# Another order ahead of the gathered rows, and the expert choices cut into pieces

## The reference

```python
# first block
xn = rms_norm(h, mix_norm_w); q, f, i, g, lru_x, lru_gate = split(xn @ w_in)
o_hg  = hgrn2_mix(q, f, i, g)      # linear attention with gates, in chunks of 32 tokens:
        # b = cumsum(log f); q*exp(b), k*exp(-b), k*exp(b_last - b); a state goes from chunk to chunk
o_lru = rglru_mix(lru_x, lru_gate) # conv of 4 taps, sigmoid gates, h_t = a_t h_{t-1} + b_t, times gelu
h += concat(o_hg, o_lru) @ w_out
h += (silu(gate) * up) @ w_down    # gate, up = split(rms_norm(h) @ w_gate_up), 2816 wide
x  = rms_norm(h)
# second block
shift1, scale1, gate1, shift2, scale2, gate2 = silu(c) @ ada_w + ada_b
h = rms_norm(x) * (1 + scale1) + shift1;  r_q, r_k, r_v, r_g, s_q, s_k, s_v = split(h @ w_in)
y_ret = group_norm(retention(rope(r_q), rope(r_k), r_v)) * silu(r_g)        # 8 heads of 64
y_sb  = rms_norm(stick_breaking(rms_norm(s_q), rms_norm(s_k), s_v))         # 8 heads of 64
x += gate1 * (concat(y_ret, y_sb) @ w_out)
h2 = rms_norm(x) * (1 + scale2) + shift2
# PEER: for each of 8 heads, 2 lists of 128 scores -> best 16 of each -> best 16 of the 256 sums
qry = h2 @ w_query; top_s, top_i = top_k(qry . sub_keys, 16)
best_s, best_c = top_k(top_s[0][:, None] + top_s[1][None, :], 16)
act = gelu(h2 . expert_down[ids]) * softmax(best_s)       # 16384 experts, 128 per token
x += gate2 * sum(act * expert_up[ids])
```

## Time and profile before

| | |
|---|---|
| median of 3 runs | 1166.53 us (1166.04 to 1167.21) |
| profiled execution, own time | 1169.27 us |
| its span, first to last instruction | 1167.4 us |
| PE busy | 1029.6 us (88%) |
| DVE busy | 856.1 us (73%) |
| ACT busy | 419.9 us (36%) |
| POOL busy | 282.2 us (24%) |
| HBM read | 376.61 MB, 324 GB/s over the span |
| mean granted TensorE clock | 0.956 of full speed |

### The profile page before, as it was taken

One profiled execution on the slowest core, in us unless ns is written; L12 is line 12 of the kernel. 1 busy time (PEld: TensorE's weight loads), 2 busy tenths in 40 slices (PEclk: granted clock), 3 DMA queues, 4 the chain that ended last, 5 costly groups with the idle time before them and its releaser, 6 DMA issues.

```text
span 1167.4 us, 14402 instructions
## 1 busy us (share of the span) xinstructions
PE 1029.6 (88%) x5158; PEld 720.7 (62%) x5158; DVE 856.1 (73%) x1784; ACT 419.9 (36%) x835; POOL 282.2 (24%) x260
## 2 busy tenths in 40 slices
PE   6999999999999998988899998787788668768887
PEld 6988999999999876975465554333233223323343
DVE  5987689998868884585658777677866776776655
ACT  4654544445446663343123322222221222222112
POOL 0000000000000000044344554544354344334430
PEclk9999999999999999999899999988898899889899
DMA  9532449978937433498899999999999999999994
GB/s 356 208 127 91 148 180 350 362 290 316 325 104 288 163 108 117 192 360 332 350 421 420 421 422 421 421 422 421 422 422 421 421 421 422 421 421 421 421 422 200
DMA packets 67895, 378.61 MB, mean 324 GB/s; under 512 B 7536, under 2 KB 7920, under 8 KB 35056
## 3 DMA queue, kind: packets, MB, share of 16 engines
q0 software_dynamic: 36864, 268.45, 55.6%
q1 hardware_dynamic: 29808, 106.09, 25.1%
q10 hardware_dynamic: 1152, 3.15, 0.8%
HBM read 376.61 MB, written 1.05 MB: 324 GB/s over the span
## 4 chain that ended last, share of the span: by engine, by line
PE 47%; DMA 30%; DVE 14%; ACT 5%; issue 4%; POOL 0%; SPq 0%; POOLq 0%; DVEq 0%; ACTq 0%
DMA xn<-in_peer,idsb 23%; PE pb L929 7%; PE pb L431 7%; PE pb L428 7%; PE pb L932 7%; DMA ring_sb<-in_peer,idsb 5%; PE pb L456 4%; DVE ring_lo L1452 3%; PE pb L813 2%; PE pb L643 2%; PE pb L884 1%; DVE ring_sb L2062 1%; PE pb L473 1%; PE pb L475 1%; PE pb L474 1%
## 5 line engine op out<-in xcount | busy, mean ns | idle before, releaser
L929 PE MATMUL pb<-ring_sb,arena 128*128 128x512 f32 x274 | 151.9, 638 | 83.1 <-ACT arena L1391 83.1
L2062 DVE CUSTOM_DVE_ANT_0 ring_sb<-ring_sb,arena 128x1024 f32<-128x1024 f32 x137 | 164.3, 1223 | 54.2 <-DMA ring_sb<-in_peer,idsb 54.1
L2134 POOL DMA_INDIRECT ring_sb<-in_peer,idsb x137 | 153.5, 1121 | 208.3 <-PE pb L932 186.3
L428 PE MATMUL pb<-xhi,whi 128*128 128x256 f32 x736 | 190.8, 293 | 0.8 <-ACT xhi L1012 0.5
L431 PE MATMUL pb<-xlo,whi 128*128 128x256 f32 x736 | 186.0, 287 | 0.5 <-DVE xlo L1671 0.3
L2134 POOL DMA_INDIRECT arena<-in_peer,idsb x38 | 40.8, 1074 | 558.8 <-DVE idsb L2041 496.6
L1386 ACT ACTIVATE arena<-arena 128x4 f32<-128x4 f32 (+2 forms) x71 | 14.5, 205 | 408.6 <-DVE arena L2062 408.6
L1452 DVE TENSOR_TENSOR ring_lo<-ring_sb,whi 128x1024 fp32r<-128x1024 f32 x126 | 147.5, 1220 | 13.3 <-ACT whi L985 13.3
L932 PE MATMUL pb<-ring_sb,arena 128*128 128x512 f32 x274 | 149.6, 629 | 0.0
L428 PEld LDWEIGHTS pb<-xhi,whi 128*128 128x128 f32 x736 | 142.6, 194 | 5.3 <-issue 3.2
L431 PEld LDWEIGHTS pb<-xlo,whi 128*128 128x128 f32 x736 | 142.7, 194 | 4.4 <-issue 2.7
(11 more groups left out here) (367 smaller groups left out, 1801.6 us busy)
## 6 DMA issues: line engine op xcount, KB each, us to landing
ring_sb<-in_ada SPq DMA_DIRECT2D x48, 512.0 KB, 5.2
ring_sb<-in_w_gu SPq DMA_DIRECT2D x44, 512.0 KB, 6.5
ring_sb<-in_w_in SPq DMA_DIRECT2D x38, 512.0 KB, 7.5
ring_sb<-in_w_down SPq DMA_DIRECT2D x22, 512.0 KB, 5.6
ring_sb<-in_w_out SPq DMA_DIRECT2D x16, 512.0 KB, 3.4
ring_sb<-in_w_q SPq DMA_DIRECT2D x8, 512.0 KB, 3.6
whi_rows<-in_w_q SPq DMA_DIRECT2D x6, 512.0 KB, 7.6
ring_sb<-in_peer,idsb POOLq DMA_INDIRECT x137, 22.5
```

The costliest lines, as they stand in the source:

```text
L428: e.matmul(o, hi_w(u)[:, c], xh(k), start=start, stop=False, skip_group_check=skip)
L929: mm = e.matmul(pb[4 + 2 * tile][:, :], dgr[col % 8], o[:, 1024:1536], start=begin, stop=end)
L2062: e.tensor_tensor_reduce(o, o, h2t[tile], 1.0, 0.0, MUL, ADD, aa[:, col:col + 1]).then_inc(*VD.up(("dot", col)))
L2134: e.indirect_dma_start(rows_at[s], None, peer, bass.IndirectOffsetOnAxis(ap=idsb[:, col:col + 1], axis=0)).then_inc(s_row[s], 16)
```

## The change

It moves work and cuts the choices; the arithmetic of the result is the same but for the order of a few sums.

- Start: ten `keep_clock` matmuls on the first input tile as soon as it is there, in place of eight behind the constants.
- `ADDED`: in n0 and n1 DVE adds slices 1 to 5, in n2 slices 1 to 3; PE adds the others by matmuls.
- First block: on DVE the memsets and the scan go ahead of the second query product, on ACT exp(b) goes last; on PE the gate matmuls go ahead of the intra-chunk ones; on DVE state steps 5 and 6 go ahead of the root's product and the LRU's product; ACT writes the high parts of the LRU's output ahead of the last sigmoid, DVE the low parts ahead of the last gate product.
- `residual`: the last two units are split after the last additions (ACT: one ahead, one behind).
- The plain sums go into the middle of U_rk's product.
- Retention: U_rg's first product goes ahead of the first group sum, its second ahead of the first mean; means and norms of the two halves are taken one by one, among the pieces of the output product; the gate is multiplied in ahead of the norm's factor (`gated`), which is then two products of 512 in place of four of 256.
- First choice: two banks, one for each list; the queries' additions go ahead of the normalised product; `match_replace` goes ahead of the first `decode`.
- Choice 1 is spread over dots 0 to 7; `second_add` stands behind dot 2, `second_norm` behind dot 6. Choices 2 to 15 become eight pieces each, one behind each of eight dots (`piece_at`).
- Groups: four of 2, 58 of 4, two of 2, twelve of 1. The places of queries and scores move by one group, scores one group closer.
- ACT loads the tables for gelu and for exp by hand in the first rows.

```diff
+        GR = [range(i, i + 2) for i in range(0, 8, 2)] + [range(i, i + 4) for i in range(8, 240, 4)]
+        GR += [range(i, i + 2) for i in range(240, 244, 2)] + [range(i, i + 1) for i in range(244, 256)]
+        second_at = {4: 0, 5: 1, 10: 2}
+        query_at = {6: (3, 0), 7: (3, 1)} | {4 * h - 8 + j: (h, j) for h in range(4, 8) for j in range(2)}
+        piece_at = {c + j: (n, j) for n, c in [(2, 16), (3, 28)] + [(n, 16 * n - 24) for n in range(4, 16)] for j in range(8)}
+        choose_at = {7: 2, 10: 3} | {4 * n - 3: n for n in range(4, 16)}
+        ADDED = {"n0": 6, "n1": 6, "n2": 4}
...
 # PE, sums
-                e.wait_ge(*AN.at((name, "sq", 7)))
-                e.matmul(pb[b][:, 0:T], c_("ones"), sq[:, 2 * T:3 * T], start=False, stop=True).then_inc(*PN.up(name))
+                for k in range(ADDED[name], KD):
+                    e.wait_ge(*AN.at((name, "sq", k)))
+                    mm = e.matmul(pb[b][:, 0:T], c_("ones"), one_(sq, sq_slot(k)), start=False, stop=k == KD - 1)
+                mm.then_inc(*PN.up(name))
...
+            e.wait_ge(s_x[0], 16)
+            keep_clock(10, hT[:, 0:128])
             e.wait_ge(s_cst, 16)
-            sums("n0", (8, 8), (AN, ("n0", "ln")))
+            sums("n0", (0, 8), (AN, ("n0", "ln")))
...
-            plain_sums()
-            gemm(U_rk[2:4], ("rk", 1), (AR, ("rk", "raw", 1)), mid=lambda: rope_turn("rk", 0))
+            gemm(U_rk[2:4], ("rk", 1), (AR, ("rk", "raw", 1)), mid=lambda: (plain_sums(), rope_turn("rk", 0)))
...
             ret_scores(2)
-            group_sum(AS, ("o", 0), AS, half(tmp, 0))
-            ret_out(0)
-            gemm(U_rg[0:2], ("rg", 0), (AR, ("rg", 0)), mid=lambda: group_sum(AS, ("o", 1), AS, half(tmp, 1)))
+            gemm(U_rg[0:2], ("rg", 0), (AR, ("rg", 0)), mid=lambda: (group_sum(AS, ("o", 0), AS, half(tmp, 0)), ret_out(0)))
+            group_sum(AS, ("o", 1), AS, half(tmp, 1))
             ret_out(2)
             ret_scores(4)
             ret_scores(6)
-            ret_mean(0)
-            ret_out(4)
+            gemm(U_rg[2:4], ("rg", 1), (VR, ("rg", 1)), mid=lambda: (ret_mean(0), ret_out(4)))
             ret_out(6)
-            ret_mean(1)
-            gemm(U_rg[2:4], ("rg", 1), (VR, ("rg", 1)), mid=ret_norms)
...
                 out_half(0, i, range(4, 8), pb[outs[i]])
+                if i == 0:
+                    ret_mean(1)
+                    ret_norm(0)
+                if i == 1:
+                    ret_norm(1)
...
 # PE, rows
                 if i == 1:
                     query_tile(2, 0)
+                    second_sums()
...
 # ACT, rows
+            e.preload_act_table_set(GELU)
             for i in range(NB + 1):
-                if i == 2:
-                    n3_root(1)
+                if i in choose_at:
+                    choose(choose_at[i])
                 if i < NB:
                     prepare(i)
                 if i == 0:
                     second_gate(range(4, 8))
+                    second_squares()
+                if i == 2:
+                    e.preload_act_table_set(LNEXP)
                     choose(1)
+                    n3_root(1)
+                    e.preload_act_table_set(GELU)
...
 # DVE
+            state_step(5)
             e.wait_ge(*AL.at("root"))
             e.tensor_tensor(la_, la_, ig_, MUL).then_inc(*VL.up("bi"))
...
             e.tensor_tensor_scan(th_, a_, la_, 0.0, MUL, ADD).then_inc(*VL.up("h"))
+            state_step(6)
...
+            def piece(n, j):
+                if j < 2:
+                    best_of_list(n, j)
+                elif j == 2:
+                    pair_up(n)
+                elif j == 3:
+                    best_first(n)
+                elif j == 4:
+                    best_second(n)
+                elif j == 5:
+                    e.wait_ge(*VT.at((n, "best", "index2")))
+                    marks(n, 0, 16)
+                elif j == 6:
+                    numbers(n, 0, 16)
+                else:
+                    gates(n)
...
             def prepare(i):
                 for col in GR[i]:
                     dot(col)
-                weigh(i)
-                if i in choose_at:
-                    choose(choose_at[i])
+                    if col == GR[i][-1]:
+                        weigh(i)
+                    if col in piece_at:
+                        piece(*piece_at[col])
```

More of the change, by code:

```diff
@@ L933, in add_rows @@
                              stop=end).then_inc(*PU.up(("row", col)))
-            scores(0, (0,))
+            for p in range(2):
+                b = where["first", p] = bank((VT, (0, p, "max2")))
+                if p == 0:
+                    e.wait_ge(s_sub, 32)
+                e.wait_ge(*VQ.at(("qry", 0, 0, p)))
+                e.matmul(pb[b][:, 0:128], qry[0][:, p * T:p * T + 128], sub[0][:, p * 128:(p + 1) * 128], start=True,
+                         stop=True).then_inc(*PQ.up(("SC", 0, 0, p)))
             rest()
@@ L1286, in ret_mean, with first_gate, ret_square @@
                 e.activation(half(yr, i), pb[4 + i][:, :], ACT.Copy).then_inc(*AR.up(("yr", i)))
-            sb_norm(0)
-            take(U_rg[0:2])
-            sb_norm(1)
-            e.wait_ge(*USED.at(U_rg[1]))
-            e.activation(half(rgs, 0), pb[where["rg", 0]][:, :], ACT.Copy).then_inc(*AR.up(("rg", 0)))
-            ret_mean(0)
-            ret_mean(1)
-            take(U_rg[2:4])
-            for i in range(2):
+            def first_gate():
+                e.wait_ge(*USED.at(U_rg[1]))
+                e.activation(half(rgs, 0), pb[where["rg", 0]][:, :], ACT.Copy).then_inc(*AR.up(("rg", 0)))
+            def ret_square(i):
                 e.wait_ge(*VR.at(("yc", i)))
@@ L1299, in act @@
                 e.activation(half(tmp, i), half(yr, i), ACT.Square).then_inc(*AR.up(("yn", "sq", i)))
+            sb_norm(0)
+            take(U_rg[0:2])
+            sb_norm(1, first_gate)
+            ret_mean(0)
+            take(U_rg[2:4])
+            e.preload_act_table_set(SIGM)
+            e.wait_ge(*VR.at(("rk", "out", 0)))
+            e.wait_ge(*AR.at(("rg", 0)))
+            e.activation(half(raw, 0), half(rgs, 0), ACT.Sigmoid).then_inc(*AR.up(("rgs", 0)))
+            ret_square(0)
+            e.wait_ge(*USED.at(U_rg[3]))
+            e.wait_ge(*VR.at(("rk", "out", 1)))
+            e.activation(half(raw, 1), pb[where["rg", 1]][:, :], ACT.Sigmoid).then_inc(*AR.up(("rgs", 1)))
+            e.preload_act_table_set(LNEXP)
+            ret_mean(1)
+            ret_square(1)
             for i in range(2):
@@ L1491, in residual @@
                 for i in range(4):
-                    if i == 3:
-                        split(la.take(us[3], name == "wo"))
+                    new = la.take(us[3], name == "wo") if i == 3 else []
                     la.used(2)
@@ L2097, in dve @@
             weigh(0)
-            best_of_pairs(1)
+            best_first(1)
             dot(2)
+            best_second(1)
+            second_add()
             dot(3)
-            decode(1, 0, 16)
             weigh(1)
-            second_add()
+            dot(4)
+            e.wait_ge(*VT.at((1, "best", "index2")))
+            marks(1, 0, 16)
+            dot(5)
+            weigh(2)
+            numbers(1, 0, 16)
+            dot(6)
+            second_norm()
+            dot(7)
+            weigh(3)
             gates(1)
-            for i in range(2, NB + 1):
+            for i in range(4, NB + 1):
                 if i < NB:
                     prepare(i)
-                if i == 2:
-                    second_norm()
-                if i == 11:
+                if i == 12:
                     e.wait_ge(*PN.at(("n3", 1)))
```

289 lines of the change are left out of this document (139 added, 150 removed).

## The result

The changed kernel took 1145.55 us (median of 4 runs, 1144.95 to 1145.82), the kernel before 1166.31 beside it (4 runs): ratio 0.982, 95% interval 0.9803 to 0.9837. The forecast was 1144 with a range of 1137 to 1156, so the time was met. The half ahead of the rows was met by its own steps, but for one stage that the sum left out. In the rows the size was met and the schedule worked out for the changed kernel came out, but the cause given for the two pauses was incomplete.

What follows compares the result with a forecast made beforehand. Ahead of the rows PE's waits and lower clock set the pace, then DMA gathers 256 rows at 2.49 us plus pauses. Gains 12.0 + 10.8 = 22.8 us off the 1166.53 median gave 1144, range 1137 to 1156.

Steps and rivals of the forecast that it cites:

- The rows' 10.8: Rows phase: of 12.3 us of pauses all but 1.5 go, a gain of 10.8 us, bounds 5 and 12.3.
- Rival A: Rows: the pauses only move, so only the 12.0 us ahead of the rows are gained, 1154.5 us; chance 0.14.
- B: Ahead of the rows: early shifts do not add up as DVE becomes the limit, 1152 to 1155.7 us; chance 0.14.
- The early part: Everything ahead of the rows: shifts that add up to 12.0 us, bounds 5.3 and 16.4.
- The start: Warm-up on the first input tile: first normalisation 2.6 us earlier, then limited by DVE's split of the first weights.
- The gates' step: Gate matmuls ahead of the intra-chunk ones need no copy by ACT: 0.8 us gained.
- The state steps: First block, steps 5 and 6 earlier on DVE: PE's 2.5 us wait and lower clock go, 3.9 us gained.
- The plain sums: Sums inside U_rk's product: the 1.5 us wait for a PSUM bank moves to the product, gain 0.
- the retention: Three waits (1.0, 1.1, 0.8 us) go, the clock stays up, two new waits of 0.45 each: net 3.7 us.
- Both pauses have one cause: Rows: places come free late because dots wait on DVE behind choice 1 and second_add, then choice 2; 12.3 us lost.
- Pauses left: First rows: 1.5 us of pause stays, since row 9's place comes free with a margin of about zero.
- Rival C: Rows: pieces between dots delay additions, the DMA pauses at each of 14 choices, 1197 us; chance 0.04 with the like.

Runs made afterwards that it cites:

- early_only: The changed kernel with the rows' part as in the kernel before, so only the part ahead of the rows changed: 1155.03 us, ratio 0.9895.
- rows_only: The kernel before with the rows' part of the change alone, everything ahead of the first query undone: 1158.36 us, ratio 0.9931.
- state_back: The changed kernel with only state steps 5 and 6 on DVE, and the LRU output's high and low halves, put back late: 1150.88 us, ratio 0.9856.
- before_again: The kernel before, unchanged, profiled a second time: profiled execution 1167.75 us.
- pairs_only: early_only with one edit, rows 4 to 7 as two groups of two and not one of four: 1155.07 us.
- later_xn: As better, with DVE's product xn of the first half also moved behind the first decode: 1154.64 us.
- fours: The changed kernel with only rows 4 to 7 as one group of four again (second_norm behind dot 7): 1152.94 us, ratio 0.987.
- dots_back: The changed kernel with only DVE's order of the first rows moved back towards the old one, groups of two kept: 1145.7 us.
- whole_choices: The changed kernel with only the pieces undone, choices 2 to 15 each one block on DVE, choice 2 behind row 19: 1146.37 us.
- better: The changed kernel with n2 adding six squares on DVE and the first choice's match_replace behind the first decode: 1145.68 us.

## Why the prediction was right, and where it was not

**The frame held.** First gather plus 256 rows at the DMA's pace plus pauses plus a fixed end: the last dot moved by 12.57 + 10.79, and early_only and rows_only show the two terms alone (by the medians 12.1 and 8.8). The forecast took 22.8 us off the median; measured are 20.8 beside it and 21.6 to 22.1 against the later series. The rows' 10.8 was read from a profile 2.7 us above the median, and is 9 by the second profile and by the medians. Rival A (pauses move) and B (early shifts don't add) fell with these two.

**The early part** came out term by term within 0.5 us, all but one. The terms that were forecast gave 13.5 us together and not 12.0, and the stage left out took 1.0 back, so that its sum came so close is in part luck. The start is bound by DVE's split, as said: it ends at 13.3 and the normalisation starts at 13.25. The gates' step gave 1.3 and not 0.8, a term too small. The state steps were both the wait and the clock: state_back takes 4.5 back. Of the other steps only this comparison of marks speaks; none was undone by itself. The plain sums gave 0, with the rope's 1.5 us at the product. In the retention the three waits went, the clock stayed at 1.00, and the two new waits of 0.4 came; 3.5 against 3.7. Its table load, 453.77 + 1.28, has the next activation at 455.07 with no idle time: the rule of the Trainium skill (ScalarE: Activation LUTs, What ACT_TABLE_LOAD costs) that a switch costs a drain of 1.38 us beside the load is not borne out by this trace either.

**One term was missing**: the FFN stage. It took 184.83 to 184.84 us in the three traces with the old early part, and 184.85 to 186.31 in the eleven with a changed one, which all run the same code in that stage: 1.0 more in the changed kernel, none in early_only, 0.7 in the mean. PE waits there for a low half (0.3, L462) and ACT for the weights' DMA (4.8 us within 175 to 215, at a DMA share of 0.96). That reaching the stage 10 us earlier uses up a lead of the weights is a guess: in the kernel before ACT waits 6.0 us for the same DMA in that window, at a share of 0.97, and PE loses nothing. The cause is open.

**In the rows the size held, and so did the schedule.** The forecast had row 2 added at 518.0 in the time of the kernel before, row 4 right behind the scores near 521.9, its dot 4.5 us and the gather of row 11 about 6 us sooner. The changed kernel, shifted back by 12.57, has 517.7 and 521.5, and 4.1 and 6.5 us.

**The step "Both pauses have one cause" failed.** For the first pause it named DVE's order of dots ahead of row 4 alone, and table loads by hand as "nothing beyond the first rows". The row is in fact held by three things in series, of which DVE's order is one: its dot, the last dot of its group, and ACT, whose activation of the group stands behind other work. The view of PE's waits over 500 to 590 of the kernel before has one line:

```profile
PE pb L929 <- ACT arena L1391: 9.4, 4, 3.9
```

In the changed kernel this is 2.5 us. The line names who comes last, not who is to blame. At row 4 of the kernel before, ACT and PE show:

```profile
524.71 1.28 ACT L1386 ACT_TABLE_LOAD   x1
526.00 0.20 ACT L1386 ACTIVATE arena<-arena 128x4 f32<-128x4 f32 x1
526.98 1.29 PE L929 MATMUL pb<-ring_sb,arena 128*128 128x512 f32 x2 [3.87 <-ACT arena L1391]
```

The last dot of the group ended at 524.1, so of PE's 3.87 us ACT itself held 1.9, and in the second profile of that kernel 0.8. The same steps in the others (us behind the first gather):

```
kernel          dot 4   last dot of its   ACT's        row 4    rows
                        group ends        activation   added    phase
before          22.35   27.0              28.9         29.9     661.7
before_again    22.5    28.3              29.05        30.0     659.8
early_only      23.3    27.9              31.5         32.5     661.6
pairs_only      22.85   25.25             29.4         30.4     660.75
later_xn        24.4    28.05             28.1         30.0     660.75
fours           18.1    26.8              26.85        27.8     660.2
dots_back       20.2    22.6              22.6         25.5     650.8
changed         18.2    21.9              22.0         24.45    650.9
```

In pairs_only the group of two is ready early and ACT serves it 4.2 us late. In fours ACT is there at once, but the group is complete only behind dot 7. In later_xn the groups are of two and ACT is there at once, but the dots themselves are late (the second query and all behind it came late too). Each of the three kernels has lost all or nearly all of the rows' gain. So no single edit carries it: groups of two alone give 0.8 us of the rows phase (pairs_only against early_only), all the rest of the rows' part without them 1.4 (fours against early_only), together 10.8 against the first profile of the kernel before; the medians give 0.0, 2.1 and 9.5 (whole against early_only). Not separated are ACT's order, its tables loaded by hand and the places of the scores, which are one group closer on PE and ACT, and how late DVE's dots may be.

For the second pause the step named the block of choice 2. That a block behind row 15 costs is so (2.2 us against the place behind row 19, with the changed rows), but cutting it into pieces is worth 0.2 us (whole_choices). With the block behind row 15 the stretch lost 2.9 to 5.0 us in the traces with the first pause and 3.2 without it; behind row 19 it lost 2.3 with it and 1.0 without. So the place did most of it, and how much the end of the first pause added is within the scatter. That one free place more is the reason is argued, not shown.

**Pauses left.** Forecast 1.5 us. By the windows shown 2.7 remain, of which 1.6 lie in the first 25 us, which hold the start of the flow itself; with the cut at 487.43 it is 1.8. Row 9's place came at 507.25 (forecast 519.8 - 12.6 = 507.2). In better the first gather came 0.5 us sooner and this place only 0.3; whether its margin is zero, as forecast, no run settles. Rival C fell: with the pieces no window behind 576 is under 420 GB/s until 1100.

## What to carry to other kernels

Before giving a stall to the engine on which the late work stands, ask for the waits of the engine that consumes it in that very window: here it named ACT with 9.4 us. Then follow the named engine one step further: at row 4 of the kernel before only 1.9 of 3.87 us were ACT's own, the rest was the wait for the dots of a group of four. Edits that each remove one of several things in series show nothing alone, so undo them one by one from the changed kernel as well as adding them to the old one, and look in the trace whether the edit gave back the whole delay that it was meant to: dots_back gave back 2.0 of 4.1 us. Here a phase that DMA bounds follows a phase bound by the engines' waits, and their gains added (12.1 + 8.8 = 20.9 against 21.6 us); each can be read from one mark in the trace.

## What the runs showed of the hardware that was not expected

The granted clock after a wait differs between executions of the same code. At the same code the granted clock over 460 to 465 was 0.71, 0.66 and 1.00 in three executions, over 110 to 120 it was 0.83, 0.83 and 0.66, which moved what follows by 1.4 to 1.6 us each time. In pairs_only it was 0.66 over 110 to 115, where early_only, with the same code and the same wait of 0.8 us ahead of it (L435), had 1.00. What decides it, no run shows. It fell after a wait of 2.5 us in state_back and of 2.8 us in better, and did not after one of 1.8 us in the changed kernel (1.00 over 520 to 540). So 1 to 1.6 us at such a place is not yet an effect of an edit; the rows phase, where it has no pauses, repeats within 0.4 us in five kernels (650.75 to 651.15: rows_only, dots_back, state_back, changed, whole_choices). With pauses it moved by 1.9 us between two executions of the kernel before.
